# Expert blocks of an MoE stage: down in the block's own step, transposes and hidden rows in halves

## What is computed

```python
def expert_block(args):
    xb, e = args                       # xb: 128 rows x 1024
    return (jax.nn.silu(xb @ w_eg[e]) * (xb @ w_eu[e])) @ w_ed[e]
```

## Time and profile before

| what | us |
|---|---|
| median of 3 runs (2868.82 to 2869.57) | 2869.02 |
| the profiled execution's own time | 2867.73 |
| its span in the trace | 2866.1 |
| mean granted clock of TensorE, share of full | 0.957 |
| expert stage, first x transpose to the next stage's first load | 1714.19 to 2817.96 |

### The profile page before, as it was taken

One profiled execution on the slowest core, in us unless ns is written; L12 is line 12 of the kernel. 1 busy time (PEld: TensorE's weight loads), 2 busy tenths in 40 slices (PEclk: granted clock), 3 DMA queues, 4 the chain that ended last, 5 costly groups with the idle time before them and its releaser, 6 DMA issues. The chain is left out here.

```text
span 2866.1 us, 28552 instructions
## 1 busy us (share of the span) xinstructions
PE 2592.7 (90%) x7895; PEld 1293.1 (45%) x7896; DVE 854.1 (30%) x2231; ACT 498.1 (17%) x982; POOL 697.3 (24%) x582
## 2 busy tenths in 40 slices
PE   5797999999995896999999939999999999999990
PEld 2344444444442473455555524444444444444440
DVE  0136665757578111233333330110011010101103
ACT  1121222222211122222222101111111111111112
POOL 0024645555464000011111111111111111211114
PEclk9898999999997998999999969999999999999995
DMA  7120111010104115322111136677756784645966
GB/s 279 59 99 26 42 47 55 33 55 33 59 30 176 54 76 212 117 74 74 59 59 59 59 116 214 193 248 230 261 180 228 244 290 132 223 143 188 340 211 264
DMA packets 153556, 397.15 MB, mean 139 GB/s; under 512 B 18498, under 2 KB 19034, under 8 KB 153482
## 3 DMA queue, kind: packets, MB, share of 16 engines
q1 hardware_dynamic: 125533, 338.28, 32.7%
q0 software_dynamic: 18336, 51.53, 7.5%
q10 hardware_dynamic: 9621, 6.51, 0.8%
HBM read 326.16 MB, written 70.35 MB: 138 GB/s over the span
## 5 line engine op out<-in xcount | busy, mean ns | idle before, releaser
L773 PE MATMUL a_psz<-W 128*128 128x512 f32 x1088 | 484.6, 599 | 1.3 <-ACT W L585 1.3
L671 DVE SCALAR_TENSOR_TENSOR yacc<-aext,pcol,yacc 128x256 f32<-128x256 f32 x928 | 369.9, 477 | 0.0
L1838 PE MATMUL e_psg<-W,e_xT 128*128 x784 | 346.4, 595 | 2.0 <-DVE e_xT L1797 2.0
L1859 PE MATMUL e_psy<-W,e_hT 128*128 x784 | 344.7, 593 | 1.0 <-ACT e_hT L1770 1.0
L1842 PE MATMUL e_psu<-W,e_xT 128*128 x784 | 344.5, 593 | 0.0
L773 PEld LDWEIGHTS a_psz<-W 128*128 128x128 f32 x1088 | 205.7, 193 | 239.2 <-issue 239.2
L555 POOL TENSOR_TENSOR a_vn<-a_vn,gv 128x512 f32<-128x512 f32 x17 | 243.1, 14303 | 15.2 <-ACT a_vn L619 15.2
L1544 PE MATMUL r_psx<-W 128*128 128x512 f32 x544 | 238.1, 596 | 0.0
L1842 PEld LDWEIGHTS e_psu<-W,e_xT 128*128 128x128 f32 x784 | 149.3, 190 | 187.2 <-issue 187.2
L1803 DVE TENSOR_TENSOR e_hb<-e_psu,e_sg 128x512 f32<-128x512 f32 x49 | 33.9, 692 | 661.4 <-PE e_psu L1842 352.8
L1518 PE MATMUL r_pss<-W,r_h2T 128*128 128x512 f32 x512 | 227.5, 598 | 1.4 <-DVE r_h2T L1390 1.4
(11 more groups left out here) (276 smaller groups left out, 2193.1 us busy)
## 6 DMA issues: line engine op xcount, KB each, us to landing
W<-in_w_expert_gate SPq DMA_DIRECT2D x32, 2048.0 KB, 12.9
W<-in_w_expert_up SPq DMA_DIRECT2D x32, 2048.0 KB, 18.2
W<-in_w_expert_down SPq DMA_DIRECT2D x32, 2048.0 KB, 22.4
W<-in_x_prompt SPq DMA_DIRECT2D x32, 512.0 KB, 3.9
x_scratch<-W SPq DMA_DIRECT2D x17, 512.0 KB, 2.9
r_x1r<-x_scratch SPq DMA_DIRECT2D x17, 512.0 KB, 4.3
x_scratch<-r_x SPq DMA_DIRECT2D x17, 512.0 KB, 2.9
h_scratch<-r_h SPq DMA_DIRECT2D x17, 512.0 KB, 2.9
```

The lines of the kernel that those rows point to most:

```text
L671: ins = dve.scalar_tensor_tensor(out=out, in0=src, scalar=w, in1=yacc[:, i, :], op0=ALU.mult, op1=ALU.add)
L773: last = pe.matmul(psz[bank][:], hT[t.par][:, k, :], w_in[:, k, COL[bank]:COL[bank] + 512], start=(k == 0), stop=(k == KD - 1))
L1838: last = pe.matmul(psg[:], xT[t.par][:, k, :], W[:, bass.ds(base + 512 * k, 512)], start=(k == 0), stop=(k == KD - 1))
L1859: last = pe.matmul(psy[:, 512 * n:512 * n + 512], hT[:, k, :], W[:, bass.ds(base + 8192 + 1024 * k + 512 * n, 512)], start=(k == 0), stop= ...
```

## The change

Steps are no longer skewed: down(b) comes in the step of gate_up(b). On PE a step is now gate_up(b), four x transposes of block b+1 (x_lo), two h transposes of b (h_lo), two x transposes (x_mid), two h transposes (h_hi), two x transposes (x_hi), down(b): seven parts in place of four, each with its `If` in the loop. The hidden rows are made in two halves of 256 columns, each with its own count of h_done. psh becomes two PSUM tensors; ACT copies the first half to hT, DVE the second, each with its own semaphore (hT_lo, hT_hi). down takes its sum over the hidden columns in two halves and waits for hT_lo, then hT_hi; both column halves of psy are open through both, so y_psum comes after three quarters of its matmuls. x_turned is counted twice a block. ACT has parts silu, hT_out, xT_out, y_evac; DVE gets one part more; POOL scatters block b in step b.

```diff
-            psh = pb("e_psh", [P, KE, P])
+            psh = [pb(f"e_psh{i}", [P, KE, P]) for i in range(2)]
...
 # POOL
-                    block_steps(pool, nb, [(2, gather), (3, fetch), (0, fetch_again), (-1, scatter)])
+                    block_steps(pool, nb, [(2, gather), (3, fetch), (0, fetch_again), (0, scatter)])
...
 # ACT
                     def hT_out(t):
-                        act.wait_ge(S["h_turned"], t.v + 1)
+                        act.wait_ge(S["h_turned"], 2 * t.v + 1)
                         act.wait_ge(S["blocks_left"], t.v + 1)
-                        act.activation(hT[:], psh[:], ACT.Copy).then_inc(S["hT_done"], 1)
+                        act.activation(hT[:, 0:2, :], psh[0][:, 0:2, :], ACT.Copy).then_inc(S["hT_lo"], 1)
...
-                    block_steps(act, nb, [(-1, hT_out), (0, silu), (1, xT_out), (-1, y_evac)])
+                    block_steps(act, nb, [(0, silu), (0, hT_out), (1, xT_out), (0, y_evac)])
...
 # DVE
-                        need(dve, S["h_turned"], t.v)
-                        dve.tensor_tensor(hb[:], psu[:], sg[:], ALU.mult).then_inc(S["h_done"], 1)
+                        need(dve, S["h_turned"], 2 * t.v)
+                        for m in range(2):
+                            c = slice(256 * m, 256 * m + 256)
+                            dve.tensor_tensor(hb[:, c], psu[:, c], sg[:, c], ALU.mult).then_inc(S["h_done"], 1)
+
+                    def hT_out(t):
+                        dve.wait_ge(S["h_turned"], 2 * t.v + 2)
+                        dve.wait_ge(S["blocks_left"], t.v + 1)
+                        dve.tensor_copy(hT[:, 2:4, :], psh[1][:, 0:2, :]).then_inc(S["hT_hi"], 1)
...
-                    block_steps(dve, nb, [(2, tokens), (0, hidden), (1, xT_out), (-1, y_evac)])
+                    block_steps(dve, nb, [(2, tokens), (0, hidden), (0, hT_out), (1, xT_out), (0, y_evac)])
...
 # PE
-                    def turn_x(t):
-                        pe.wait_ge(x_here[t.par], 16 * (t.half + 1))
-                        need(pe, S["xT_done"], 2 * t.v)
-                        for k in range(KD):
+                    def turn_x(t, ks):
+                        if ks[0] == 0:
+                            pe.wait_ge(x_here[t.par], 16 * (t.half + 1))
+                            need(pe, S["xT_done"], 2 * t.v)
+                        for k in ks:
                             last = pe.transpose(psx[:, k, :], xg[t.par][:, P * k:P * k + P], ident[:])
-                        last.then_inc(S["x_turned"], 1)
+                        if ks[-1] in (3, 7):
+                            last.then_inc(S["x_turned"], 1)
...
-                    def turn_h(t):
-                        pe.wait_ge(S["h_done"], t.v + 1)
-                        need(pe, S["hT_done"], t.v)
-                        for k in range(KE):
-                            last = pe.transpose(psh[:, k, :], hb[:, P * k:P * k + P], ident[:])
+                    def turn_h(t, m):
+                        pe.wait_ge(S["h_done"], 2 * t.v + m + 1)
+                        need(pe, S["hT_hi" if m else "hT_lo"], t.v)
+                        for k in (2 * m, 2 * m + 1):
+                            last = pe.transpose(psh[m][:, k - 2 * m, :], hb[:, P * k:P * k + P], ident[:])
                         last.then_inc(S["h_turned"], 1)
...
                     def down(t):
                         e, base = weights(t)
                         pe.wait_ge(down_here, 16 * e + 16)
-                        pe.wait_ge(S["hT_done"], t.v + 1)
                         need(pe, S["y_done"], 2 * t.v)
-                        for n in range(2):
-                            for k in range(KE):
-                                last = pe.matmul(psy[:, 512 * n:512 * n + 512], hT[:, k, :],
-                                                 W[:, bass.ds(base + 8192 + 1024 * k + 512 * n, 512)], start=(k == 0), stop=(k == KE - 1))
-                            last.then_inc(S["blocks_left" if n else "y_psum"], 1)
-                    turn_x(fixed(0))
-                    block_steps(pe, nb, [(-1, turn_h), (0, gate_up), (1, turn_x), (-1, down)])
+                        for m in range(2):
+                            pe.wait_ge(S["hT_hi" if m else "hT_lo"], t.v + 1)
+                            for n in range(2):
+                                for k in (2 * m, 2 * m + 1):
+                                    last = pe.matmul(psy[:, 512 * n:512 * n + 512], hT[:, k, :],
+                                                     W[:, bass.ds(base + 8192 + 1024 * k + 512 * n, 512)], start=(k == 0), stop=(k == KE - 1))
+                                if m:
+                                    last.then_inc(S["blocks_left" if n else "y_psum"], 1)
+                    turn_x(fixed(0), (0, 1, 2, 3))
+                    turn_x(fixed(0), (4, 5, 6, 7))
+                    block_steps(pe, nb, [(0, gate_up), (1, x_lo), (0, h_lo), (1, x_mid), (0, h_hi), (1, x_hi), (0, down)])
```

More of the change, by code:

```diff
@@ L1666, in build @@
             psu = pb("e_psu", [P, DE])
-            psh = pb("e_psh", [P, KE, P])
+            psh = [pb(f"e_psh{i}", [P, KE, P]) for i in range(2)]
             psy = pb("e_psy", [P, D])
-            names = "token_done stoken_done x_turned xT_done gate_psum up_psum silu_done h_done h_turned hT_done y_psum y_done blocks_left".split()
+            names = "token_done stoken_done x_turned xT_done gate_psum up_psum silu_done h_done h_turned hT_lo hT_hi y_psum y_done blocks_left".split()
             S = {n: sem("e_" + n) for n in names}
@@ L1734, in gather @@
                         pool.wait_ge(S["token_done"], t.v + 1)
-                        need(pool, S["x_turned"], t.v - 1)
+                        need(pool, S["x_turned"], 2 * (t.v - 1))
                         settle(pool)
@@ L1763, in silu @@
                         act.wait_ge(S["gate_psum"], t.v + 1)
-                        need(act, S["h_done"], t.v)
+                        need(act, S["h_done"], 2 * t.v)
                         act.activation(sg[:], psg[:], ACT.Silu).then_inc(S["silu_done"], 1)
                     def hT_out(t):
-                        act.wait_ge(S["h_turned"], t.v + 1)
+                        act.wait_ge(S["h_turned"], 2 * t.v + 1)
                         act.wait_ge(S["blocks_left"], t.v + 1)
-                        act.activation(hT[:], psh[:], ACT.Copy).then_inc(S["hT_done"], 1)
+                        act.activation(hT[:, 0:2, :], psh[0][:, 0:2, :], ACT.Copy).then_inc(S["hT_lo"], 1)
                     def xT_out(t):
-                        act.wait_ge(S["x_turned"], t.v + 1)
+                        act.wait_ge(S["x_turned"], 2 * t.v + 1)
                         need(act, S["up_psum"], t.v - 1)
@@ L1794, in xT_out @@
                     def xT_out(t):
-                        dve.wait_ge(S["x_turned"], t.v + 1)
+                        dve.wait_ge(S["x_turned"], 2 * t.v + 2)
                         need(dve, S["up_psum"], t.v - 1)
@@ L1819, in _, with x_lo, x_mid, x_hi @@
                     pe.sem_inc(S["blocks_left"], 1)
-                    def turn_x(t):
-                        pe.wait_ge(x_here[t.par], 16 * (t.half + 1))
-                        need(pe, S["xT_done"], 2 * t.v)
-                        for k in range(KD):
-                            last = pe.transpose(psx[:, k, :], xg[t.par][:, P * k:P * k + P], ident[:])
-                        last.then_inc(S["x_turned"], 1)
+                    def turn_x(t, ks):
[3 more added lines that the diff above has]
+                        for k in ks:
+                            last = pe.transpose(psx[:, k, :], xg[t.par][:, P * k:P * k + P], ident[:])
+                        if ks[-1] in (3, 7):
+                            last.then_inc(S["x_turned"], 1)
+                    def x_lo(t):
+                        turn_x(t, (0, 1, 2, 3))
+                    def x_mid(t):
+                        turn_x(t, (4, 5))
+                    def x_hi(t):
+                        turn_x(t, (6, 7))
                     def weights(t):
@@ L1839, in gate_up @@
                         last.then_inc(S["gate_psum"], 1)
-                        need(pe, S["h_done"], t.v)
+                        need(pe, S["h_done"], 2 * t.v)
                         for k in range(KD):
@@ L1843, in gate_up, with h_lo, h_hi @@
                         last.then_inc(S["up_psum"], 1)
-                    def turn_h(t):
-                        pe.wait_ge(S["h_done"], t.v + 1)
-                        need(pe, S["hT_done"], t.v)
-                        for k in range(KE):
-                            last = pe.transpose(psh[:, k, :], hb[:, P * k:P * k + P], ident[:])
+                    def turn_h(t, m):
[3 more added lines that the diff above has]
+                            last = pe.transpose(psh[m][:, k - 2 * m, :], hb[:, P * k:P * k + P], ident[:])
                         last.then_inc(S["h_turned"], 1)
+                    def h_lo(t):
+                        turn_h(t, 0)
+                    def h_hi(t):
```

(1 more changed line is left out.)

## The result

The changed kernel takes 2997.7 us (median of 4 runs, 2996.38 to 2998.97) where the kernel before takes 2868.92 beside it: a ratio of 1.0449, 95% interval 1.0431 to 1.0467. It is 129 us slower. The profiled execution took 2998.97 us with a span of 2997.4.

A forecast was written before the change was run, and what follows sets the result against it. PE's own work was taken to bound the stage. Block gaps 97.7 + 6.6 + 2.0 less 1.4 (104.9), plus 8.5 at the end, on 2867.73, and 1.3 for the median, gave 2982 us; range 2955 to 3014.

The forecast's parts named there:

- The bound and the sign: Expert stage: PE's own work bounds it, no matmul is removed, so new gaps make it slower (chance 0.97).
- The sequencer is held by an h wait: PE, each block: branches, register ops and loads run only after the wait; stall 2.12 plus 0.10 restart, 2.22 us.
- the bound where only the loads are held: Lower case: branches and semaphore ops pass a waiting transpose, loads do not; 1.65 us a block for all 49, 2957 us.
- U: Time zero of a loop block's count: the start of the first of its x transposes on PE.
- The first four blocks: Blocks 0 to 3, which have no branches: 1.65 us each, 6.6 us together.
- The end: After the last down: PE skips 119 parts and becomes the last, 38.9 us for 30.35, cost 8.5 us.
- The clock: Rival: PE's gaps lower the granted clock, 1.7 us a fall; in every block 3057 us; chance of over half the blocks 0.06.
- one block of six: Clock falling in one of six blocks: 12 us more, 2994 us, counted inside the range.
- rival 1: PE's sequencer passes the h wait, loads hidden, down waits only for hT_lo: 2905 us, chance 0.07.

The follow-up runs named there:

- e1: The changed kernel with down, y_evac and scatter working on the block before again, h transposes kept in their own block's step: 3003.27 us, ratio 1.0471.
- e6: e5 with the two loads of weights() run once, at the start of a step, for both gate_up and down: 2896.48 us, ratio 1.0097.
- e7: The changed kernel with the hidden-row multiply in one instruction of 512 columns again, both halves signalled at its end: 3028.92 us, ratio 1.0558.
- e4: The kernel before, order, skew and waits kept, with PE's list cut into seven parts, each with its branch: 2876.34 us, ratio 1.0027.
- e3: The kernel before with the loop's turns read from the number of blocks, so no empty steps: 2859.55 us, ratio 0.9967.
- e2: The changed kernel with twelve more unused 128x128 transposes behind x_hi, in the idle gap before down: 2987.42 us, ratio 1.0412.
- e5: The changed kernel with the loop's turns read from the number of blocks, so no empty steps: 2981.52 us, ratio 1.0392.

## Why the prediction was right, and where a term was off

- **The bound and the sign.** PE was full, and only a gap could change the time. Shown by the waits after.
- **The sequencer is held by an h wait, and with it branches, register ops and loads (2.12 us of the 2.22 a block).** Right, and the central step. e1 shows that the gap before down doesn't depend on fresh data, e6 that it goes when the loads stand before the wait: some 70 us of gaps, where 72 were expected, and 13 of the clock, of 85 in all. The rows of 2091.4 to 2098.4 show the hold at h_lo itself. e7 shows that the branches behind h_lo's wait are held as well; by the bound where only the loads are held (2957) nothing would have moved.
- **The size of it.** 24.19 us measured in the block shown, 24.22 on average in the loop without the falls, 24.14 forecast (21.92 + 2.22). The prediction's own terms for down's start add to U + 3.46 and not 3.43 (1.22 + 0.14 + 2.0 + 0.1), and the upper end of its range to 3012, not 3014; measured is U + 3.48. One piece was mis-sized: the first half reached PE at U + 0.84, not U + 0.74, since VectorE's multiply starts 0.36 after U (2097.49 to 2097.85) where it started 0.26 after it in the earlier trace rows. The probable reason: the count of h transposes to be waited for is now twice the block number, and VectorE's sequencer makes that number only after the wait for up_psum has ended, in front of the multiply. Its row in the window 2121.8 to 2122.1 of the changed kernel:

```profile
L76 DVEq ALU_OP  x1: 45/45/45, 2121.9 to 2121.9; - x1
```

  No run takes this op away, so its part in the 0.10 is argued and not shown. Nor is it the hold that PE has: here the wait for up_psum is an instruction of VectorE's sequencer itself (an EVENT_SEMAPHORE at 2121.9), and the register op merely follows it. The path from h_lo's release to down was 2.64 for an estimated 2.69, which gave back half of the 0.10. Over all blocks the gaps come to 108.2 for 104.9.
- **The first four blocks** at 1.65: the three distances between their downs are 1.55 to 1.66 longer than before.
- **The end.** 8.5 us forecast, 8.5 measured; last down to the next stage 38.9 forecast, 38.8 measured. That PE's skips take over from POOL's DRAIN is confirmed by e4 with the old order. But what I expected of POOL in e3, that without its skips the DRAIN follows the last scatter at once, was wrong: e3 shows that the landing of the scatter lies hidden under those skips.
- **The clock.** I had it as a rival with the right price (1.7 us a fall) and a wrong chance for the middle: I kept the forecast at no fall, with one block of six as the upper part of the range. It came in one block of seven: 11.9 us, and that is nearly the whole of the 15 us by which 2982 lies under 2997.7. The two gaps of 2.01 us in the earlier trace rows, one followed by a fall, had said as much; an expected value of some falls belonged in the sum. e2, with the gap filled, and e6, with it gone, show that the falls come with the idle gap.
- **Hidden passing of the wait (rival 1, 2905)** did not occur. The rule of the Trainium skill (Advanced Engine Details and Errata, section Sequencer Loop) speaks of engine instructions: they wait in a queue, and other engine instructions can be read and queued while the sequencer's microcode executes. It doesn't name register loads or branches, so the prediction read more into it than it states. What the runs show for those is the hold: nothing of them ran in the 6.6 us in front of 2098.33, and e1 and e6 decide against rival 1.
- **The rest.** 2.7 us lie before the stage, which the change doesn't touch. With the 11.9 and the 3.3 that makes 17.9 on the profiled execution. Of that 2.6 are hidden in the medians: the forecast had added 1.3 for a median above the profiled execution, and after the change the median lay 1.3 below it. That part of the closeness is luck.

What stays open: what decides which block gets a fall of the clock. The runs show that no fall comes with the gap filled or short, 7 with gaps of 0.24 and 1.55 us a block (9 in e1, with nearly the same gaps), 16 with 0.58 and 1.57. They also show that the falls, once begun, come at even distances, in every fifth or sixth block in the changed kernel and e5, every fourth or fifth in e1, every second or third in e7. A down with a fall has the same gap before it as one without (1.57 us at 2002.47 in the changed kernel, 1.57 at 2100.94 in e5), so that gap alone doesn't single out the block.

## What to carry to other kernels

A wait on the engine that bounds a kernel costs more than the data's delay: it takes away the lead of its sequencer, and every branch, address computation and register load between that wait and the next long instruction is then paid in full. Before moving a wait next to its producer, list what the sequencer runs behind it (the trace has it, in rows that no busy time counts), and put the loads ahead of the wait. A loop that runs to the largest possible count isn't free either: here its empty steps cost 9 us before and 16 after the change.

## What the runs showed of the hardware that I had not expected

- A register op, load or branch of PE's sequencer starts with the waiting weight load ahead of it, not before: the load of 1733.6 with the release of 1733.61, the branch of 2098.3 with the release of 2098.33. Two dependent loads with their register ops and checks take 1.4 us (from 2099.1 to 2100.5), as long as 13 transposes of 128x128; to move them took 1.47 us off a block (e5 to e6).
- The granted clock falls with idle gaps of about 1.6 us that come every 24 us: in 7 blocks of 48, and in 16 of 48 when the small gap before them grew from 0.24 to 0.58 us. A fall lasts 3.4 us and costs 1.7.
- A branch that skips its part takes PE's sequencer 0.202 to 0.217 us, one that doesn't 0.065 to 0.068.
- POOL's DRAIN at the end of this stage takes 4.64 to 4.68 us. In e3 it starts only after the last scatter has landed, 6.5 us after that started, since the kernel waits for the landing in front of it.
